# Last expert product: two tiles of experts at a time by seven block products

## The reference, cut to what matters

```python
def peer_experts(xc, idx, gates, u, v):
    u_sel = jnp.take(u, idx, axis=0)
    act = jax.nn.gelu(jnp.einsum("chkd,cd->chk", u_sel, xc))
    v_sel = jnp.take(v, idx, axis=0)
    return jnp.einsum("chk,chkd->cd", act * gates, v_sel)
...
h = h + peer_layer(hn, peer_w_q[l], peer_sub_keys[l], peer_u[l], peer_v[l])
h = rms_norm_2(h, final_norm_g)
```

## Time and profile before

| | us |
|---|---|
| median of 3 runs | 1355.31 |
| lowest and highest | 1353.93, 1356.35 |
| profiled execution | 1356.69 |
| its span | 1354.8 |
| PE busy in the span | 1330.0 |
| DVE, ACT, POOL busy | 950.2, 768.5, 442.6 |

### The profile page before, as it was taken

One profiled execution on the slowest core, in us unless ns is written; L12 is line 12 of the kernel. 1 busy time (PEld: TensorE's weight loads), 2 busy tenths in 40 slices (PEclk: granted clock), 3 DMA queues, 4 the chain that ended last, 5 costly groups with the idle time before them and its releaser, 6 DMA issues.

```text
span 1354.8 us, 26681 instructions
## 1 busy us (share of the span) xinstructions
PE 1330.0 (98%) x9169; PEld 1209.8 (89%) x9169; DVE 950.2 (70%) x1751; ACT 768.5 (57%) x1379; POOL 442.6 (33%) x254
## 2 busy tenths in 40 slices
PE   7999999999998999999999999999999999999997
PEld 7998979988978988999999999999988888888886
DVE  4777667656676974899989888889545555555555
ACT  6545454444556355477767676676545555555554
POOL 1100424000025661079887666766720000000000
PEclk9989999999999999999999999999999999999999
DMA  8533035555553444555554444444455555555553
GB/s 303 165 109 110 32 125 194 188 190 192 188 173 127 155 141 140 164 166 184 187 185 157 156 144 155 155 151 147 165 190 188 186 186 186 187 187 187 190 188 130
DMA packets 62465, 225.29 MB, mean 166 GB/s; under 512 B 7200, under 2 KB 7712, under 8 KB 62000
## 3 DMA queue, kind: packets, MB, share of 16 engines
q1 hardware_dynamic: 60656, 218.36, 48.6%
q10 hardware_dynamic: 1728, 5.84, 1.2%
HBM read 223.12 MB, written 1.05 MB: 165 GB/s over the span
## 4 chain that ended last, share of the span: by engine, by line
PE 95%; DVE 2%; issue 1%; ACT 1%; DMA 0%; POOL 0%; SPq 0%; POOLq 0%; DVEq 0%; ACTq 0%
PE bank L533 83%; PE bank L1072 3%; PE bank L634 1%; PE bank L780 1%; PE bank L766 1%; PE bank L590 1%; PE bank L1027 1%; DVE arena L2083 0%; PE bank L935 0%; DMA cols<-in_cols 0%; PE bank L565 0%; PE bank L515 0%; PE bank L950 0%; PE bank L682 0%; PE bank L595 0%
## 5 line engine op out<-in xcount | busy, mean ns | idle before, releaser
L1165 ACT ACTIVATE w_hi<-ring 128x1024 fp32r<-128x1024 f32 x414 | 439.2, 1061 | 515.5 <-PE bank L533 327.4
L1717 DVE TENSOR_TENSOR w_lo<-ring,w_hi 128x1024 fp32r<-128x1024 f32 x259 | 317.4, 1226 | 274.3 <-ACT w_hi L1165 269.7
L533 PE MATMUL bank<-hT_hi,w_hi 128*128 128x256 f32 (+2 forms) x1696 | 420.6, 286 | 0.0
L533 PE MATMUL bank<-hT_lo,w_hi 128*128 128x256 f32 (+2 forms) x1696 | 412.9, 282 | 0.0
L1669 POOL TENSOR_TENSOR w_lo<-ring,w_hi 128x1024 fp32r<-128x1024 f32 x128 | 310.4, 2427 | 158.3 <-ACT w_hi L1165 158.1
L533 PEld LDWEIGHTS bank<-hT_lo,w_hi 128*128 128x128 f32 x1696 | 320.4, 189 | 0.4
L533 PEld LDWEIGHTS bank<-hT_hi,w_hi 128*128 128x128 f32 x1696 | 318.9, 188 | 0.4
L533 PE MATMUL bank<-hT_hi,w_lo 128*128 128x256 f32 (+2 forms) x1696 | 234.8, 280 | 0.0
L533 PEld LDWEIGHTS bank<-hT_hi,w_lo 128*128 128x128 f32 x1696 | 215.9, 189 | 0.0
L533 PE MATMUL bank<-w_hi,wgt_lo 128*128 128x512 f32 x504 | 199.6, 396 | 0.0
L533 PE MATMUL bank<-w_hi,wgt_hi 128*128 128x512 f32 x504 | 199.3, 395 | 0.0
(11 more groups left out here) (360 smaller groups left out, 1683.2 us busy)
## 6 DMA issues: line engine op xcount, KB each, us to landing
ring<-in_stream SPq DMA_DIRECT2D x414, 512.0 KB, 3.5
arena<-in_rows ACTq DMA_DIRECT2D x1, 1536.0 KB, 10.8
consts<-in_consts ACTq DMA_DIRECT2D x1, 1152.0 KB, 5.6
arena<-in_keys ACTq DMA_DIRECT2D x1, 1024.0 KB, 6.1
h<-in_x SPq DMA_DIRECT2D x2, 256.0 KB, 3.8
h<-in_x ACTq DMA_DIRECT2D x2, 256.0 KB, 4.3
arena<-in_rows ACTq DMA_DIRECT2D x1, 512.0 KB, 3.5
out_h<-arena SPq DMA_DIRECT2D x2, 256.0 KB, 2.1
```

What stands on the lines that cost most here:

```text
L533: mm = nc.tensor.matmul(o, a, b, start=first and not low_part and xp is x[0], stop=last and low_part)
L1165: nc.scalar.activation(w_hi[:, g % S, :], ring[:, g % R, :], ACT.Copy).then_inc(hi_done, 1)
L1717: nc.vector.tensor_tensor(w_lo[:, g % S, :], ring[:, g % R, :], w_hi[:, g % S, :].bitcast(F32), ALU.subtract).then_inc(lo_done, 1)
```

## The change

From tile 26 on, every seventh and eighth tile (26 and 27, 33 and 34, ... 117 and 118) are taken together as a pair: 2 x 2 blocks of activations (two halves of tokens, two tiles of experts) times 2 x 2 blocks of the matrix (two tiles of experts, two halves of features). A pair is multiplied in the Winograd form of Strassen's method, with seven block products instead of eight, each in the same three high and low parts. Five plain tiles stand between two pairs and are done as before. The pair's products that serve several outputs accumulate in banks 4 to 7 over all pairs; two of them go straight to banks 0 and 1, and one to bank 2.

For each pair VectorE makes four sums of blocks of the matrix (T1 to T4) and four of the activations (S1, X2, X3, X4), ScalarE the high parts and VectorE the low parts of these and of three blocks of the matrix. This work is spread over steps 2 to 5 (and 6) after the previous pair's first tile, that is over the preparation of the five plain tiles before the pair. The pair's tiles don't go through the ring: SP loads them into a buffer of their own. After the last pair VectorE adds and subtracts banks 4 to 7 to h with eight additions of 512 columns, at tiles 120 to 123, and ScalarE copies one bank. The loops end after 16 tiles (18 on ScalarE and VectorE); the rest is written out. The zero matmuls are dropped, the first tile starts the banks itself.

```diff
+PLAIN_BETWEEN = 5
+FIRST_PAIR = 26
+PAIRS = list(range(FIRST_PAIR, N_KEYS - 7, 2 + PLAIN_BETWEEN))
+PAIR_OF = {n + j: k for k, n in enumerate(PAIRS) for j in range(2)}
+V_LOOPED = 4
+def pair_step(n):
+    k = sum(q <= n for q in PAIRS)
+    return k, n - (PAIRS[k - 1] if k else PAIRS[0] - PLAIN_BETWEEN - 2)
...
+            # SP
+            def pair_load(k):
+                first, second = (stream_in[G_V + PAIRS[k] + j] for j in range(2))
+                sp_eng.dma_start(pair_w[:, W11:W12 + 1:W12 - W11, :], first.rearrange("p (c n) -> p c n", c=2))\
+                      .then_inc(pair_loaded, 16)
+                sp_eng.dma_start(pair_w[:, W21:W22 + 1, :], second.rearrange("p (c n) -> p c n", c=2))\
+                      .then_inc(pair_loaded, 16)
+            for n in PLAIN:
...
+                k = PAIR_OF.get(n - 1)
+                if k is not None and k + 1 < len(PAIRS):
+                    sp_eng.wait_ge(pair_lo, pair_lo0 + 1 + 4 * k)
+                    pair_load(k + 1)
                 sp_eng.wait_ge(lo_done, g - R + 1)
+                sp_eng.dma_start(ring[:, g % R, :], stream_in[G_V + n]).then_inc(slot_full[g % R], 16)
...
+            # PE: high is two matmuls, low is one
+                pe.wait_ge(wgt_out, n0 + 1)
+                pe.wait_ge(pair_hi, pair_hi0 + 1 + 4 * k)
+                pe.wait_ge(pair_lo, pair_lo0 + 1 + 4 * k)
+                high(4, a11, pair_w_hi[:, W11, :])
+                low(4, a11, pair_w_lo[:, W11, :]).then_inc(pair_used, 1)
+                pe.wait_ge(pair_lo, pair_lo0 + 4 + 4 * k)
+                high(5, s1, pair_t_hi[:, T1, :])
+                low(5, s1, pair_t_lo[:, T1, :])
+                high(7, x3, pair_t_hi[:, T3, :])
+                low(7, x3, pair_t_lo[:, T3, :]).then_inc(pair_used, 1)
+                pe.wait_ge(wgt_out, n0 + 2)
+                high(0, a12, pair_w_hi[:, W21, :])
+                low(0, a12, pair_w_lo[:, W21, :])
+                high(1, x4, pair_w_hi[:, W22, :])
+                low(1, x4, pair_w_lo[:, W22, :]).then_inc(pair_used, 1)
+                high(6, x2, pair_t_hi[:, T2, :])
+                low(6, x2, pair_t_lo[:, T2, :])
+                high(2, a22, pair_t_hi[:, T4, :])
+                low(2, a22, pair_t_lo[:, T4, :]).then_inc(pair_used, 1)
-            open_sums()
...
+            # ScalarE
+            def w_copy(k):
+                act.wait_ge(pair_loaded, pair_loaded0 + 32 * (k + 1))
+                pair_free(k, 3)        # pair k - 1 has reached its third pair_used
+                pair_copy(pair_w_hi[:, :, :], pair_w[:, W11:W22 + 1, :])
+            def t_copy(k, first, sums, part):
+                act.wait_ge(pair_sums, pair_sums0 + sums + 6 * k)
+                pair_free(k, part)
+                pair_copy(pair_t_hi[:, first:first + 2, :], pair_t[:, first:first + 2, :])
+            # step 2: w_copy(k), t_copy(k, T1, 1, 2); step 3: t_copy(k, T2, 4, 4); step 4: x_copy(k)
+            for n in range(V_LOOPED * PEER_BODY + 2, N_KEYS):
+                if n in G_OF and n - 2 not in PAIR_OF:
+                    hi(G_OF[n])
+                rows_high(n)
+                if n in PAIR_OF:
+                    hi(G_OF[n + 2])
+                k, step = pair_step(n)
+                if k < len(PAIRS):
+                    pair_steps(step, k)
...
+            # VectorE, step 2: first_sums; step 3: further_sums; step 4, 5: t_low; step 6: low part of X
+            def first_sums(k):
+                dve.wait_ge(pair_loaded, pair_loaded0 + 32 * (k + 1))
+                pair_sum(pair_t[:, T1:T3 + 1, :], pair_w[:, W11:W22 + 1:2, :], over(pair_w[:, W12, :], 2), ALU.add)
+            def further_sums(k):
...
+                pair_sum(pair_t[:, T2, :], pair_t[:, T1, :], pair_w[:, W22, :], ALU.add, k, 1)
+                pair_sum(pair_x[:, X3:S1 + 1, :], over(a21, 2), both, ALU.subtract)
+                pair_sum(pair_t[:, T4, :], pair_t[:, T2, :], pair_w[:, W21, :], ALU.add, k, 2)
+                pair_sum(pair_x[:, X2, :], a11, pair_x[:, S1, :], ALU.subtract, k, 3)
+                pair_low(k, 1, pair_w_lo[:, :, :], pair_w[:, W11:W22 + 1, :], pair_w_hi[:, :, :])
+                pair_sum(pair_x[:, X4, :], a12, pair_x[:, X2, :], ALU.subtract, k, 5)
+            for n in range(V_LOOPED * PEER_BODY + 2, N_KEYS):
+                if n in G_OF and n - 2 not in PAIR_OF:
+                    lo(G_OF[n])
+                wgt_low(n, act_all[:, n, :], n)
+                if n in PAIR_OF:
+                    lo(G_OF[n + 2])
+                k, step = pair_step(n)
+                if k < len(PAIRS):
+                    pair_steps(step, k)
+                else:
+                    pair_ends(step)
```

More of the change, by code:

```diff
@@ L60 @@
 G_V = G_PEER + N_KEYS
+PLAIN_BETWEEN = 5
+FIRST_PAIR = 26
+PAIRS = list(range(FIRST_PAIR, N_KEYS - 7, 2 + PLAIN_BETWEEN))
+PAIR_OF = {n + j: k for k, n in enumerate(PAIRS) for j in range(2)}
+PLAIN = [n for n in range(N_KEYS) if n not in PAIR_OF]
+G_OF = {n: G_V + at for at, n in enumerate(PLAIN)}
+G_LAST = G_V + len(PLAIN)
+V_LOOPED = 4
+def pair_step(n):
+    k = sum(q <= n for q in PAIRS)
+    return k, n - (PAIRS[k - 1] if k else PAIRS[0] - PLAIN_BETWEEN - 2)
 ROUTED = 44
@@ L240, in two_stack_kernel @@
         u_free = 84
-        taken[0] = max(taken[0], u_free * T)
+        act_blocks = arena[:, :].rearrange("p (e b) -> p e b", b=P)
+        taken[0] = 0
+        pair_w = area(4, HALF)
+        pair_w_hi, pair_w_lo = split_area("pair_w", 3, HALF)
+        pair_x_hi, pair_x_lo = split_area("pair_x", 4, P)
+        assert taken[0] <= (FIRST_PAIR - 2) * T
+        pair_t = consts[:, C_TRI:C_TRI + 4 * HALF].rearrange("p (a n) -> p a n", a=4)
+        pair_t_hi, pair_t_lo = (a.rearrange("p k n -> p (k n)")[:, 0:4 * HALF].rearrange("p (a n) -> p a n", a=4)
+                                for a in (hT_hi, hT_lo))
+        pair_x = idxT.rearrange("p a n -> p (a n)")[:, 0:4 * P].rearrange("p (a n) -> p a n", a=4)
+        X3, S1, X2, X4 = range(4)
+        T1, T3, T2, T4 = range(4)
+        W11, W21, W22, W12 = range(4)
+        taken[0] = u_free * T
         scores = area(NT * NHH, N_KEYS)
@@ L1091, in wgt_lhs, with pair_products, high, low @@
                 return wgt_hi[:, j % 2, t * P:(t + 1) * P], wgt_lo[:, j % 2, t * P:(t + 1) * P]
-            open_sums()
-            with pe.Fori(0, N_KEYS // PEER_BODY - 1) as i:
+            def pair_products(k):
+                n0, first, last = PAIRS[k], k == 0, k == len(PAIRS) - 1
+                def high(b, x, w):
+                    nc.tensor.matmul(bank[b][:, :], x[0], w, start=first and b >= 4, stop=False)
+                    nc.tensor.matmul(bank[b][:, :], x[1], w, start=False, stop=False)
+                def low(b, x, w):
+                    return nc.tensor.matmul(bank[b][:, :], x[0], w, start=False, stop=last and b >= 4)
+                def rows_part(j, t):
+                    o = slice(t * P, (t + 1) * P)
+                    return wgt_hi[:, (n0 + j) % 2, o], wgt_lo[:, (n0 + j) % 2, o]
+                a11, a12, a22 = rows_part(0, 0), rows_part(1, 0), rows_part(1, 1)
+                x3, s1, x2, x4 = ((pair_x_hi[:, n, :], pair_x_lo[:, n, :]) for n in range(4))
+                pe.wait_ge(wgt_out, n0 + 1)
[17 more added lines that the diff above has]
+                low(2, a22, pair_t_lo[:, T4, :]).then_inc(pair_used, 1)
@@ L1095, in _, with plain_tile @@
+            def plain_tile(n):
+                w = tile(G_OF[n])
+                pe.wait_ge(wgt_out, n + 1)
+                row_tile(w, lambda t: wgt_lhs(n, t), 0, n == 0, False)
+            for n in range(PEER_BODY):
+                plain_tile(n)
+            with pe.Fori(1, V_LOOPED) as i:
                 for j in range(PEER_BODY):
@@ L1099, in _ @@
                     row_tile((g % S, i * PEER_BODY + (g + 1)), lambda t: wgt_lhs(j, t), 0, False, False)
[L1100 to L1104, removed]
+            for n in range(V_LOOPED * PEER_BODY, N_KEYS - 2):
+                if n in PAIRS:
+                    pair_products(PAIR_OF[n])
+                elif n in G_OF:
+                    plain_tile(n)
+            closing_rows([(G_OF[n], [wgt_lhs(n, t) for t in range(NT)], (wgt_out, n + 1))
                           for n in (N_KEYS - 2, N_KEYS - 1)], 0, 3)
@@ L1527, in _, with rows_free, rows_high, pair_copy @@
             act.wait_ge(late_out, N_KEYS - PAIRED)
-            with act.Fori(0, N_KEYS // PEER_BODY - 1) as i:
+            def rows_free(n):
+                if n - 2 in G_OF:
+                    act.wait_ge(tiles_done, G_OF[n - 2] + 1)
+                else:
+                    k = PAIR_OF[n - 2]
+                    act.wait_ge(pair_used, pair_used0 + 4 * k + (1 if n - 2 in PAIRS else 4))
+            def rows_high(n):
+                rows_free(n)
+                wgt_high(n, n)
+            def pair_copy(o, src):
+                nc.scalar.activation(o, src, ACT.Copy).then_inc(pair_hi, 1)
+            def pair_free(k, part):
+                if k:
```

(78 more changed lines are left out.)

22 lines of the change are left out of this document (17 added, 5 removed).

## The result

The changed kernel takes 1373.7 us in the median of 4 runs (1372.51 to 1376.4) against 1355.83; the ratio is 1.0136, 95% interval 1.0118 to 1.0155. It is slower, by 1.4%. The forecast was 1374.6.

The account below looks back on a forecast made before the run. TensorE bounds the kernel, with VectorE only 0.88 us ahead. Terms: -9.8 - 0.7 + 14 x 2.0 + 1.8 = +19.3 us, giving 1376.0 profiled and 1374.6 median; range 1366 to 1385.

Parts of the forecast that it names:

- What goes: PE: 21 matmuls a pair instead of 24, 0.70 us less, 9.8 us over 14 pairs; zero matmuls 0.7 us.
- Prices: VectorE's new sums cost what w_lo does, 1.14 us per 1024 elements, 0.61 per 512; ScalarE copies 1.03 per 1024.
- (b): Rival, VectorE: the new sums are cheap, at the lower bound of 0.61 of their price; +7 us, 1363; chance 4%.
- (c): Rival, VectorE: everything a little dearer, 0.05 us on each of eight instructions; stall 2.6 us, +8.4, 1383; chance 8%.
- Step 1: ScalarE: W copy starts 3.7 us behind the pair's first matmul; T copy ends at 6.2, wgt_hi of n0+3 at 6.6.
- Steps 2 and 3: VectorE: wgt_lo of n0+3 starts at 6.65, in time; further sums and W's low part follow, free at 10.65.
- Steps 4 and 5: ScalarE's w_hi of n0+4 ends at 10.8, then VectorE's w_lo, wgt_lo done 12.4; PE stalls 2.0 us a round.
- First preparation: Before the first pair: tile 22 is 1.3 us late, tile 23 2.5; together 3.8 instead of 2.0, +1.8 us.
- (a): Rival: the average decides; queues even out, PE never waits, 1344.8 us; chance 6%.
- (d): Rival, TensorE: clock falls to 1.2 instead of 2.4 GHz behind each of 14 stalls; +31 us, 1406; chance 6%.
- What lies hidden: Pair transfers cost nothing to 1 us a round; unrolled code zero to 3 us, taken as 0; closing additions nothing.

Follow-up runs that it names:

- e1: Changed kernel with all loads, sums and splits of pairs 1 to 13 left out, their products reading pair 0's operands; 1349.26 us, ratio 0.9945 to before.
- e3: Changed kernel with ScalarE's second T copy one step later, behind w_hi and wgt_hi of tile n0+4 (n0 the pair's first tile); 1372.13 us, ratio 1.0125.
- e4: Changed kernel with W's low part made of only 8 of each 512 columns for pairs 1 to 13; 1372.57 us, ratio 1.0125.
- e5: Changed kernel with the edits of e3 and e4 together; 1352.31 us, ratio 0.9977 to before.
- e2: Changed kernel with all eight sums in the preparation's step 2 on VectorE, only W's low part left in its step 3; 1346.68 us, ratio 0.9934.
- e7: Changed kernel with the edits of e2 and e3 together and the first pair's preparation spread over steps 0 to 6; 1345.29 us, ratio 0.9929.
- e6: Changed kernel with eight plain tiles between pairs instead of five, first pair at 29, 10 pairs; 1368.43 us, ratio 1.0097.
- e8: e7 with four plain tiles between pairs, 16 pairs instead of 14; 1347.13 us, ratio 0.9949 to before.
- e9: e8 with the ring transfer of tile n0+2 issued ahead of the next pair's two transfers instead of behind; 1343.65 us, ratio 0.9918.

## Why the prediction was right, step by step

The mechanism, the place, the releaser and the direction came out as forecast; 1374.6 against 1373.7. That the two agree within 0.9 us is partly luck: the forecast was 19.3 us more than before, the medians differ by 17.9, and the median of before had moved from 1355.31 to 1355.83 with a fourth run.
- *What goes*: 0.75 us a pair, shown by e1's rounds; 0.70 forecast.
- *Prices*: the new sums cost what w_lo does: 128x1024 took 1218 ns, 128x512 684, 128x256 417, 128x128 281, 128x1536 1749. Rivals (b) and (c) fall with these rows.
- *Step 1*: W copy 3.74 us behind the pair's first matmul, 3.7 forecast. *Steps 2 and 3*: wgt_lo of n0+3 started at 6.51, not 6.65, and T2 to X4 followed without a pause.
- *Steps 4 and 5*: w_lo of n0+4 started at 10.55, not 10.8, since ScalarE's copies in front of another instruction cost less here than I had read between w_hi and wgt_hi: 0.95 and 0.97 us for 1024 elements and not 1.03, 1.39 for 1536 and not 1.46. The stall with its restart was 20.73 - 18.85 = 1.88 us instead of 2.0, and the round 20.73 instead of 20.9. This is the mis-sized term: 13 x 0.17 = 2.2 us. The prediction had ScalarE's line end 0.15 us after VectorE's (10.8 against 10.65); they ended within 0.1 us of each other, and e3, e4 and e5 show it.
- *First preparation*: gaps of 1.12 and 2.13 us, with 0.24 us each for the restart and the modelled end 3.7 us; 3.8 forecast. e2 and e7 take it away in two parts.
- *(a), the average decides*: refuted for this kernel by the result and by e6, and reached by a change of order alone in e7 (1345.3 against 1344.8 that (a) gave).
- *(d), the clock*: not behind each stall, but once. In the profiled execution, the slowest of the four, the windows (last columns: granted clock, DMA share, GB/s) behind the 2.13 us gap at tile 23 read

```profile
1056.00:1058.00 2.00, 0.43 (x2) 1.00 0.36 102
1058.00:1060.00 2.00, 2.00 (x7) 0.58 1.02 401
1060.00:1062.00 2.00, 2.00 (x7) 0.56 0.92 369
1062.00:1064.00 2.00, 2.00 (x10) 1.00 1.01 408
```

  and that tile took 1061.99 - 1057.57 = 4.42 us instead of 2.88: 1.5 us. The granted clock lay near the lower of its two levels (1.2 of 2.4 GHz) for these 4 us. The transfers are not the reason: at 1062 to 1064 they were as dense and the clock was full. e1, e3, e4 and e5 also have two gaps there and no slow matmuls behind them (36 in 8.63 us); e6 has slow ones. Why the clock fell in two of these six kernels' profiled executions stays open. The 13 gaps of the later rounds are followed by 36 matmuls in 8.64 us, at the full clock, so a slow start behind every stall, which by the prediction's price would have cost 31 us, did not happen. In the Trainium skill ("TensorE: Matmul & The Clock Gate", the section on HAM oscillation) the kernel whose every stretch starts slow waits 3 to 5 us for its data each time. The prediction stretched that case to gaps of 2 us; no gap of the last product here lasts 3 us, so no run tests it.
- *What lies hidden*: the transfers cost nothing in the changed kernel, nor in e7, where PE has no gap and ScalarE never waits for the ring. The bound that I had set at "nothing to 1 us a round" became real in e8, with 3 us in 16 rounds. Ring transfers took 5.1 us from issue to landing in 1060 to 1340 us after, against 3.4 before, and 6.5 in e8.

The sum for the profiled execution, from the first matmul of the product to the closing rows: before 1342.07 - 989.09 = 352.98, after 1361.58 - 989.53 = 372.05, 19.07 more. By its terms: 13 rounds at 20.73 - 19.60 = 14.7, the first pair -0.7 + 3.7 = 3.0, the slow tile 1.5: 19.2. The slow tile, which the forecast did not hold, made up for 1.5 of the 2.2 us by which the rounds were shorter. The zero matmuls' 0.7 us lie in front of this stretch. From the start of the last group of the product before it to the first matmul of this one it took 989.09 - 987.46 = 1.63 us before and 989.53 - 988.59 = 0.94 after, so they were won:

```profile
987.46 1.10 PE L533 MATMUL bank<-hT_hi,w_lo 128*128 128x256 f32 x8
...
988.59 1.10 PE L595 MATMUL bank<-hT_hi,w_lo 128*128 128x256 f32 x8
...
989.53 0.39 PE L595 MATMUL bank<-w_hi,wgt_hi 128*128 128x512 f32 x1
```

The execution after reached this place 1.13 us later, and its end took 0.3 us longer. With these two the 19.1 and the -0.7 give the difference of the spans, 1374.6 - 1354.8 = 19.8. What made these 1.4 us is not shown.

## What to carry to other kernels

When work is added to in-order queues that feed a full engine, don't stop at the busy share of a round: write down when each consumer's operand leaves the queue, and compare it with the lead (here 0.9 us) that the feeding engine has. The same 2.0 us of sums (T2 to X4) helped to cost 1.88 us a round in one place and cost nothing one step earlier, where the engine stood waiting (e2: rounds as in e1). Where two queues arrive together, shortening one alone shows nothing; test both before calling either harmless, and don't trust a releaser's name where two events end at nearly the same moment.

## What was not expected of the hardware

A copy of 1024 elements on ScalarE directly in front of another instruction occupies 0.95 us of its line in the unrolled code (1118.53 to 1119.47), not 1.03 as in the looped code (1010.94 to 1011.97 before). The kernel before has it too, in its last tiles outside the loop (1338.59 to 1339.55), where I had not looked. And the transfers of 512 KB into the ring, now issued in bunches with the pairs' between them, took 5.1 to 6.5 us from issue to landing in the median instead of 3.4, while the stretch's mean rate hardly changed (187 GB/s before, 181 in e8). It was not this alone that made ScalarE wait: in e9 they still took 5.5 us, and the waits were gone because the transfer of tile n0+2 was issued earlier. How much of the delay came from the late issue and how much from the transfers in front is not separated by these runs.
